# Scratch of the router moved out of the third down buffer, three weight loads queued earlier, one gather for the first two expert blocks, and the index table between the halves of the first gate product

## What is computed

```
for layer in (0, 1):
    x = x + mixer(rms_norm(x))                 # pooling, then attention
    h = rms_norm(x)                            # rows "xn", 544 x 1024
    grp = argmax(h @ w_r1 + b_r1)              # 4 groups
    top2 = top_k(softmax(group's 8 logits), 2) # two experts a token, with gates
    for e in range(32):                        # the rows of expert e, in blocks
        xb = h[tokens of e]
        y[tokens of e] += gate * ((silu(xb @ w_gate[e]) * (xb @ w_up[e])) @ w_down[e])
    x = x + y
```

## Time and profile before

| | |
|---|---|
| median of 3 runs | 1380.27 us (1378.42 to 1382.09) |
| the profiled execution | 1383.74 us, of which the span from first to last instruction is 1381.9 us |
| PE busy | 1324.4 us, 96% of the span |
| DVE, ACT, POOL busy | 571.6, 299.2, 124.3 us |
| mean granted PE clock | 0.988 of full speed |
| DMA | 459.61 MB, mean 333 GB/s |

### The profile page before, as it was taken

The page is one execution under the profiler, slowest core; times in us unless marked ns, Lnnn a source line. Parts: engine busy times, 40 slices in busy tenths (PEclk is TensorE's granted clock), DMA queues, the critical chain, the costliest instruction groups (busy, mean ns, idle before and its releaser), DMA issues.

```text
span 1381.9 us, 19949 instructions
## 1 busy us (share of the span) xinstructions
PE 1324.4 (96%) x7564; PEld 666.8 (48%) x7564; DVE 571.6 (41%) x1057; ACT 299.2 (22%) x638; POOL 124.3 (9%) x201
## 2 busy tenths in 40 slices
PE   8989999999999999999998999989999999999998
PEld 6743344333443334778776644643434433334333
DVE  4643344433334333654416643453333433333333
ACT  3311111111111113343326443211111111111111
POOL 1010000000000001033323220000000000000000
PEclk9999999999999999999999999999999999999999
DMA  9689999999999998212137322799999999999995
GB/s 358 247 346 427 427 426 426 426 428 429 427 428 426 428 425 337 77 61 84 43 103 262 107 54 69 316 368 407 428 425 427 428 426 428 428 428 428 427 424 242
DMA packets 51504, 459.61 MB, mean 333 GB/s; under 512 B 7885, under 2 KB 9165, under 8 KB 25594
## 3 DMA queue, kind: packets, MB, share of 16 engines
q1 hardware_dynamic: 38894, 425.35, 73.6%
q0 software_dynamic: 9904, 25.05, 5.7%
q10 hardware_dynamic: 2652, 8.45, 1.7%
HBM read 455.42 MB, written 11.26 MB: 338 GB/s over the span
## 4 chain that ended last, share of the span: by engine, by line
PE 90%; DMA 3%; issue 3%; DVE 3%; ACT 1%; SPq 0%; POOL 0%; POOLq 0%; DVEq 0%; ACTq 0%
PE ps L1858 32%; PE ps L1889 11%; PE ps L1867 9%; PE ps L1868 8%; PE ps L2283 4%; PE ps L1698 3%; PE ps L1700 3%; PE ps L1699 3%; PE ps L1850 2%; PE ps L1694 2%; DMA nat<-xn,gcol 1%; PE ps L1770 1%; PE ps L1782 1%; PE ps L2217 1%; PE ps L2233 1%
## 5 line engine op out<-in xcount | busy, mean ns | idle before, releaser
L1467 DVE TENSOR_TENSOR x<-x,ps 128x1024 f32<-128x1024 f32 (+1 forms) x150 | 177.7, 1216 | 226.3 <-PE ps L1889 225.3
L1858 PE MATMUL ps<-ring,xT 128*64 128x512 f32 x352 | 159.4, 602 | 9.7 <-issue 8.1
L1858 PE MATMUL ps<-pair,xT 128*64 128x512 f32 x352 | 160.8, 607 | 5.6 <-issue 5.6
L1481 DVE SCALAR_TENSOR_TENSOR nat<-nat,slot_gate,ps 64x256 f32<-64x256 f32 x128 | 86.1, 672 | 193.5 <-ACT nat L988 163.6
L1859 PE MATMUL ps<-pair,xT 128*64 128x512 f32 x352 | 160.9, 607 | 0.0
L1889 PE MATMUL ps<-y_parts,hot 64*128 64x512 f32 (+1 forms) x1200 | 160.3, 401 | 0.0
L1859 PE MATMUL ps<-ring,xT 128*64 128x512 f32 x352 | 159.6, 602 | 0.0
L1858 PE MATMUL ps<-third_pair,xT 128*64 128x512 f32 x320 | 148.1, 612 | 10.0 <-issue 10.0
L1859 PE MATMUL ps<-third_pair,xT 128*64 128x512 f32 x320 | 148.3, 612 | 0.0
L1868 PE MATMUL ps<-qk,hidT 128*64 128x512 f32 x320 | 144.9, 595 | 0.0
L1867 PE MATMUL ps<-qk,hidT 128*64 128x512 f32 x320 | 144.8, 595 | 0.0
(11 more groups left out here) (243 smaller groups left out, 1804.2 us busy)
## 6 DMA issues: line engine op xcount, KB each, us to landing
qk<-in_moe_w_down SPq DMA_DIRECT2D x40, 2048.0 KB, 30.7
ring<-in_moe_w_down SPq DMA_DIRECT2D x22, 2048.0 KB, 29.1
ring<-in_moe_w_gate SPq DMA_DIRECT2D x20, 2048.0 KB, 25.9
ring<-in_moe_w_up SPq DMA_DIRECT2D x20, 2048.0 KB, 30.6
pair<-in_moe_w_gate SPq DMA_DIRECT2D x20, 2048.0 KB, 25.7
pair<-in_moe_w_up SPq DMA_DIRECT2D x20, 2048.0 KB, 30.2
third_pair<-in_moe_w_gate SPq DMA_DIRECT2D x20, 2048.0 KB, 24.8
third_pair<-in_moe_w_up SPq DMA_DIRECT2D x20, 2048.0 KB, 29.3
```

Of the source, the lines that this page charges most:

```text
L1467: return V.tensor_tensor(x[0:n, i, :], x[0:n, i, :], ps[0:n, bank:bank + 2, :].rearrange("p b c -> p (b c)"), ALU.add)
L1481: last = V.scalar_tensor_tensor(out=out[u * BLK:(u + 1) * BLK, :].rearrange("s (k p) -> s k p", k=n), in0=act_rows[:, u * n:(u + 1) * n, : ...
L1858: mm(ps[BLK:P, GU_BANK, :], rows, gate[:, at], start=(k == 0), stop=(k == KT - 1))
```

## The change

- `slot_rows` moves to the second 4 KB of `nat`, `index_rows` and `tmp2` into `gain`, `tmp` into `ffn_gain`; the third down buffer is no longer touched by the router.
- Layer 0: down of blocks 1 and 2 is queued as soon as the pooling mixer is through (`x_mixed`). Layer 1: up and down of block 2 are queued right behind its gate.
- Blocks 0 and 1 come by one gather of 128 rows and one `pair_transposes`; ACT copies both.
- The product for `index_ps` stands between the halves of block 0's gate and up; `gate_table` stays behind them, and waits for both copies to `xT` (its PSUM bank is the one that the transposes of block 1 use).
- In `gather_pair` the gather waits for one count of `xT_ps` less.

```diff
@@ -248,16 +248,18 @@
         r["M"] = rounded("chosen_rows", "nat", NT, NEXP)
         for name in ("extra", "incl", "offs"):
             r[name] = scratch("nat", NEXP)
-        r["S"] = rounded("slot_rows", "qk", PT, BLK)
-        r["Vi"] = rounded("index_rows", "qk", 2, NT, NB)
-        r["tmp"] = scratch("qk", max(2 * PT * NEXP, NEXP * STEPS, OVF * NEXP))
-        r["tmp2"] = scratch("qk", max(PT * NB, OVF * NEXP))
+        r["S"] = nc.alloc_sbuf_tensor_at("slot_rows", [P, PT, BLK], F32R, offset=nat_at + 4 * D)[:, :, :]
+        r["Vi"] = nc.alloc_sbuf_tensor_at("index_rows", [P, 2, NT, NB], F32R, offset=gain_at)[:, :, :, :]
+        r["tmp2"] = gain[:, PT * NB:PT * NB + max(PT * NB, OVF * NEXP)]
+        assert PT * BLK <= D and PT * NB + max(PT * NB, OVF * NEXP) <= D
         r["bias"] = sb("router_bias", [P, NR])[:, :]
         LOGIT_COLS = 104
         rw_all = sb("rw", [P, KT * NR + LOGIT_COLS - NR])
         rw = rw_all[:, 0:KT * NR].rearrange("p (k c) -> p k c", k=KT)
         ffn_gain_at = -(-nc.sbuf_base // 32) * 32
         ffn_gain = sb("ffn_gain", [P, D])
+
+        r["tmp"] = ffn_gain[:, 0:max(2 * PT * NEXP, NEXP * STEPS, OVF * NEXP)]
 
         hot = [nc.alloc_sbuf_tensor_at(f"hot{u}", [P, T], F32R, offset=(ffn_gain_at, gain_at, xT_at, nat_at + 16 * D)[u])[:, :]
                for u in range(4)]
@@ -585,24 +586,22 @@
                     load_gate(l, 1, 1)
                     load_up(l, 1, 1)
 
+                    sp.wait_ge(x_mixed[0], NT)
+                    load_down(l, 1, 1)
+                    load_down(l, 2, 2)
                     sp.wait_ge(hT_ps, NT)
-                    sp.wait_ge(xn_stored[l], 16 * NT)
                 else:
 
                     sp.wait_ge(att_y, 2 * NT)
                     load_gate(l, 1, 1)
                     load_up(l, 1, 1)
-                    sp.wait_ge(xn_stored[l], 16 * NT)
+                sp.wait_ge(xn_stored[l], 16 * NT)
 
                 sp.wait_ge(logit_ps, 2 * (l + 1))
                 load_gate(l, 2, 2)
-                if l == 0:
-                    load_up(l, 2, 2)
-                sp.wait_ge(first_in[l], 16)
-                if l == 0:
-                    load_down(l, 1, 1)
-                else:
-                    load_up(l, 2, 2)
+                load_up(l, 2, 2)
+                if l == 1:
+                    load_down(l, 2, 2)
 
                 sp.wait_ge(half_gu_ps, l + 1)
                 for to, w in ((gate_slots[0], wg), (up_slots[0], wu)):
@@ -612,9 +611,6 @@
                              weights(wg, 3 + l * NEXP)[:, SLOT // 2:SLOT]).then_inc(gate_in[0], 16)
                 sp.dma_start(up_slots[0][:, SLOT // 2:SLOT],
                              weights(wu, 3 + l * NEXP)[:, SLOT // 2:SLOT]).then_inc(up_in[0], 16)
-
-                sp.wait_ge(table_sb, l + 1)
-                load_down(l, 2, 2)
 
                 def body(b, turn, s):
 
@@ -701,7 +697,7 @@
                 pool.wait_ge(gathered[l], m * 16)
                 pool.tensor_copy(gcol[:, :], idx_gather[:, bass.ds(m, 1)]).then_inc(gcol_set[l], 1)
 
-                pool.wait_ge(xT_ps[l], m + 1)
+                pool.wait_ge(xT_ps[l], m)
                 pool.wait_ge(gcol_set[l], m + 2)
                 pool.sem_inc(wait_carrier, 1)
                 rows_in(l, xg, gcol[:, :]).then_inc(gathered[l], 16)
@@ -716,10 +712,8 @@
                 pool.wait_ge(zeroed, l + 1)
 
                 pool.wait_ge(xn_stored[l], 16 * NT)
-                pool.wait_ge(gcol_set[l], 1)
-                rows_in(l, xg[0:BLK, :], gcol_first[0][:, :]).then_inc(first_in[l], 16)
                 pool.wait_ge(gcol_set[l], 2)
-                rows_in(l, xg[BLK:P, :], gcol_first[1][:, :]).then_inc(gathered[l], 16)
+                rows_in(l, xg, gcol[:, :]).then_inc(gathered[l], 16)
 
                 pool.wait_ge(table_sb, l + 1)
                 gather_pair(l, 1)
@@ -943,14 +937,15 @@
                 store_row(0, i - 1)
                 first_chunks(0, i - 1)
 
-            def xT_first(l, b):
-
-                act.wait_ge(xT_ps[l], b + 1)
-                act.activation(xT[:, b, :], ps[:, XT_BANK, :], ACT.Copy).then_inc(xT_sb[l], 1)
+            def xT_first(l):
+
+                act.wait_ge(xT_ps[l], 1)
+                act.activation(xT[:, 0, :], ps[:, XT_BANK, :], ACT.Copy).then_inc(xT_sb[l], 1)
+                act.activation(xT[:, 1, :], ps[:, Y_BANK, :], ACT.Copy).then_inc(xT_sb[l], 1)
 
             def xT_pair(l, half):
 
-                act.wait_ge(xT_ps[l], half + 3)
+                act.wait_ge(xT_ps[l], half + 2)
                 act.activation(xT[:, 1, :], ps[:, Y_BANK, :], ACT.Copy).then_inc(xT_sb[l], 1)
                 act.activation(xT[:, 0, :], ps[:, XT_BANK, :], ACT.Copy).then_inc(xT_sb[l], 1)
 
@@ -973,7 +968,7 @@
                 act.activation(y_high[v], ps[:, bank, :], ACT.Copy).then_inc(y_hi[l], 1)
 
             def experts(l):
-                xT_first(l, 0)
+                xT_first(l)
 
                 def body(b, par, half, stage):
                     if stage >= 2:
@@ -986,9 +981,7 @@
 
                         act.wait_ge(hidden_sb[l], b)
                     act.activation(silu, ps[BLK:P, GU_BANK, :], ACT.Silu).then_inc(silu_sb[l], 1)
-                    if stage == 0:
-                        xT_first(l, 1)
-                    elif par:
+                    if par:
                         xT_pair(l, half)
 
                 blocks(act, body)
@@ -1375,7 +1368,7 @@
 
                 dve.wait_ge(first_ps, l + 1)
                 for u in range(FIRST):
-                    V.tensor_scalar(gcol_first[u][:, :], ps[0:BLK, FIRST_BANK, u:u + 1], PAD, None,
+                    V.tensor_scalar(gcol[u * BLK:(u + 1) * BLK, :], ps[0:BLK, FIRST_BANK, u:u + 1], PAD, None,
                                     ALU.add).then_inc(gcol_set[l], 1)
                 link(V.tensor_tensor(tmp[:, 0, :, :], chosen_rows, bc(const("iota_expert"), sp, 1), ALU.mult))
                 link(V.reduce_sum(r["exp"], tmp[:, 0, :, :], AX.X))
@@ -1824,11 +1817,14 @@
                     last = mm(out, slots[:, m, :], rows[:, m, :], start=(m == 0), stop=(m == PT - 1))
                 return last
 
-            def tables(l):
+            def index_table(l):
 
                 pe.wait_ge(slots_ready, 3 * l + 2)
                 table(ps[0:BLK, INDEX_BANK, 0:NB], r["S"],
                       r["Vi"].rearrange("p k i b -> p (k i) b")).then_inc(index_ps, 1)
+
+            def gate_table(l):
+
                 pe.wait_ge(slots_ready, 3 * l + 3)
                 table(ps[0:BLK, TABLE_BANK, 0:NB], f32(r["S"]),
                       r["Vg"].rearrange("p k i b -> p (k i) b")).then_inc(table_ps, 1)
@@ -1939,10 +1935,10 @@
                     pe.sem_inc(wait_carrier, 1)
                     if stage == 0:
                         gate_up(par, gate_slots[s], up_slots[s], range(KT // 2)).then_inc(half_gu_ps, 1)
+                        index_table(l)
                         gate_up(par, gate_slots[s], up_slots[s], range(KT // 2, KT)).then_inc(gu_ps, 1)
-                        tables(l)
-                        pe.wait_ge(gathered[l], 16)
-                        block_transposes(1).then_inc(xT_ps[l], 1)
+                        pe.wait_ge(xT_sb[l], 2)
+                        gate_table(l)
                     elif not par or stage == 1:
                         gate_up(par, gate_slots[s], up_slots[s]).then_inc(gu_ps, 1)
                     else:
@@ -1969,8 +1965,8 @@
                         down_block(b - 1, (s - 1) % BUFFERS, turn - (s == 0), stage - 1)
 
                 keep_busy(6, SPARE_BANK, ident, some)
-                pe.wait_ge(first_in[l], 16)
-                block_transposes(0).then_inc(xT_ps[l], 1)
+                pe.wait_ge(gathered[l], 16)
+                pair_transposes().then_inc(xT_ps[l], 1)
                 for b in range(BLOCKS_PEELED):
                     if b == 1:
 
```

9 lines of the change are left out of this document (4 added, 5 removed).

## The result

| | before | changed |
|---|---|---|
| median, same chip | 1380.62 us | 1395.49 us (1390.37 to 1395.95) |
| ratio | | 1.0101, 95% interval 1.0073 to 1.0128 |
| profiled execution, span | 1383.74, 1381.9 us | 1390.37, 1388.5 us |

A forecast was written before the change was run, and what follows sets the result against it. It took the stream of weight loads to set each layer's end; +4.3 us (layer 1) and +0.7 (layer 0) made +5.0, a median of 1385.3 us from 1380.27, range 1379 to 1390.

The forecast's parts named there:

- Fair turns between the queues: Layer 1's first gather gets half of 423 GB/s and lands at 911.3; sum -3 to -4 us, 1376.8; 1 in 10.
- forecast +4.3: Layer 1: gate of block 5 lands at 962.1 instead of 957.8, the first gather running under load; bounds +2.0 and +5.6.
- The clock was put at 1.7 us: Layer 1, block 0: a slow clock behind PE's idle stretch of 6.5 us costs 1.7 us; bounds 0 and 1.7.
- 3.9 had been forecast: Layer 1, gate of block 4's issue to gate of block 5's landing: 23.6 us instead of 27.5, 3.9 less.
- forecast +0.7: Layer 0: gather late by 1.5 us less 0.8 for the clock; bounds -1.7 and +4.4.
- So 0 to 2.7 us late; I take 1.5: Layer 0: gather lands at 78.4 to 81, where PE's first transposes are at 78.25 before the change.
- minus 0.8 for the clock: Layer 0, 86 to 100 us: half of the 1.7 us slow clock goes, as the index table leaves that stretch.
- rival (3): Layer 0 at its bound like layer 1, with late stores and loads and slow clock: +8.7 us, 1389.0; 3 in 20.
- that shift: Whole kernel: a profiled execution takes 3.5 us over the median, the same before and after the change.

The follow-up runs named there:

- experiments 1 and 2: Changed kernel with early loads held until first gather lands in layer 1, 0, both: 1.0019, 1.0043, 0.9985; kernel before with early loads and moved tables: 1.0061.
- experiment 4: Changed kernel with PE's dummy products ahead of the first transposes lengthened from 6 to 10 (layer 0) and 13 (layer 1): 1392.78 us, 1.0089.

## Why the prediction was wrong

**What held.** The direction and the mechanism: the first gather of layer 1 under load took 10.4 us where 10.5 was taken, and the early loads are most of the loss (experiments 1 and 2); PE's wait for it 6.84 (6 said, transposes 6.5 later); full rate, then a hole ahead of block 3's halves and one ahead of gate of block 4; no wait for the next gather ahead of block 0's down product; from gate of block 5 on the same length as before (434.69 and 434.48 us in the first pair). Fair turns between the queues, the faster rival, fell: it had 5.3 us for the 128 rows, which took 10.4, and even 64 rows took 8.5 to 10.7.

**Layer 1, forecast +4.3, found +5.9.** Two sizes were short. The first transposes came 18.9 us behind gate of block 2 where it was 11.7, so 7.2 us later and not 6.5: the gather that waits for both columns was issued 8.4 us behind that gate, not 7.6. The clock was put at 1.7 us; block 0's half product shows 2.5 (experiment 4). So gate of block 4 came 9.8 us later than before instead of 8.2. From there to the end it was 4.1 us shorter (3.9 had been forecast), since the hole ahead of gate of block 5 is gone (254 GB/s at 948 to 950 before, 426 and more from 952 to 958 now): 5.7 in this pair. Over four executions it is 8.9 later and 3.0 shorter, 5.9.

**Layer 0, forecast +0.7, found +4.9: the step that failed.** It read "So 0 to 2.7 us late; I take 1.5", for the first transposes, minus 0.8 for the clock. Seen from the mixer's last rows they came at 78.19 - 49.78 = 28.4 instead of 24.2 us: 4.2 late (4.2 to 4.5 over four), outside the bounds. Two sizes in it were short, about 1 us each. The last store took 9.4 us, so that gate of block 2 came at 64.38 + 4.25 = 68.6 on the old scale, where the range ended at 67.5. And its two loads, put at 12.5 us at that end (67.5 to 80), took 13.5, near the 13.6 that the prediction itself had for two such loads: they ended at 82.1 and not by 80. That the gather cannot take much longer than the load beside it held: it took 8.0 us and landed 0.3 behind it, at 82.4 where the bound was 81. The clock's sign was wrong as well: behind the wait of 4.1 us the clock is 0.50 (80 to 84 in the first profile), and over four executions the window of layer 0 loses 2.4 us more than before, where -0.8 was taken and +1.7 was the bound. This was rival (3), layer 0 at its bound as layer 1, with 3 in 20; its price of 8.7 was still 2.1 under the 10.8 of the profiles.

**Between 10.8 and 14.** The profiled execution of before was 3.5 us over its median, and I gave that shift to both kernels. It does not carry over: the four of before lie on average 2.4 us over the medians beside them (1383.6 against 1381.2), the four of the changed kernel 1.9 us under theirs (1393.8 against 1395.7). The granted clock of the timed executions says what the sample missed. In the 90 of before that were timed beside the experiments the span averages 1379.5 us at a clock of 0.9885, in the 12 of the changed kernel 1392.5 us at 0.9839: 13.0 us apart (14 by the medians). The profiled four of each have 1381.8 at 0.9868 and 1391.6 at 0.9845: 9.8 apart, or 10.8 at an equal start. Over the 90 the span grows by 1.1 us for each 0.001 that the clock lacks, over the 12 by 1.4; by these slopes, an estimate, some 2.7 of the missing 3.2 us go with the clock: the profiled executions of before had more slow time than most, those of the changed kernel a little less. The timed ratio's interval reaches from 10.2 to 18.4 us and holds the 10.8; the parts timed one by one, -2.1 + 8.0 + 4.7, give 10.6. Why the clock falls in one of several like places stays open.

## What to carry to other kernels

A load that is "held back for nothing" may be what keeps the queue empty for a short transfer on the critical path: before queueing it early, list each small transfer (stores that a signal waits for, gathers) that will then run beside it, and price each by the rows of its like under load, not by its bytes. A late store can also do its harm through the loads that wait for it: in layer 0 the gather was issued in time, but block 2's loads had been pushed beside it. To keep loads flowing, cut the one behind the hole in halves and queue it earlier in PE's own order, instead of ahead of the rows; here that gave some 3 us, not clear of the noise.

## What the runs showed of the hardware

- The gather's duration depended on the traffic beside it far more than on its size: 64 rows 3.0 to 3.9 us and 128 rows 3.4 to 4.0 with few loads about, 8.5 to 10.7 and 10.3 to 10.9 beside full loads (8.0 to 8.9 in layer 0, where the loads ended just before it). The Trainium skill ("DMA: Bandwidth & Descriptors", section "Queues, rings and completion order") has each engine take turns between its queues by packets; with turns of equal bytes the prediction worked out 5.3 us for 128 rows, and these runs don't show that.
- A store of 128 KB behind one of 512 KB on ACT's queue took 1.9 us with no loads about, 5.8 to 6.0 beside one load of 2 MB, and 9.4 to 10.4 beside two; the 512 KB store ahead of it 2.6, 8.1 to 8.3 and 10.8 to 12.1. In layer 1 the last store ran beside loads in the kernel before already: it took 9.8 us and landed at 898.2, when gate of block 2 was issued.
- Dummy products through a wait kept PE's clock at 1.00 once, and the half-clock stretch appeared 10 us later instead.
- One kernel, four executions: the mixer's last rows of layer 0 come nearly 6 us apart (49.7 to 55.5 us), with a granted clock of 1.00 in the early ones and 0.88 to 0.92 in the late ones over 8 to 50 us.
